# Sixteen neighbourhood heads: score terms stacked on 96 rows, and a mix whose output is feature by token

## The chip, the core and the metric

The kernel runs on one core of one Trainium2 chip. The metric is the device time of one execution, in microseconds (us), as the median of several runs. Engines are named PE (TensorE), ACT (ScalarE), DVE (VectorE), POOL (GpSimd) and SP (SyncE, which issues the weight loads).

## The reference, cut to what matters

The program is a two-block network on 256 tokens of 1024 features, in float32: retention, dilated attention and two feed-forward layers in the first block; a mixer (long convolutions on 512 features, neighbourhood attention on the other 512), a feed-forward layer, a Fourier mix and an eight-expert layer in the second. Only the neighbourhood attention is changed:

```python
def one_row(r):                                  # 16 heads of 32 features, 4 rows of 64 tokens, 256 context keys
    s_loc = einsum('bhjqd,bhrjkd->bhjqrk', q_r, k_r) * scale + bias
    s_loc = where(col_ok, s_loc, NEG_INF)
    s_ctx = einsum('bhjqd,bhcd->bhjqc', q_r, k_ctx) * scale
    p = softmax(concatenate([s_loc, s_ctx]))
    o = einsum('bhjqrk,bhrjkd->bhjqd', p_loc, v_r) + einsum('bhjqc,bhcd->bhjqd', p_ctx, v_ctx)
```

## The kernel before

Every float32 matrix is held in two parts, a high and a low one (`_hi`, `_lo`), and a product of two matrices is three products on PE (`mm3`): high by high, high by low, low by high. ACT makes a high part by copying, DVE makes the low part by subtracting the high one. Weights come in blocks of 1 MB on SP's queue; `ahead` (L1604 on ACT, L2164 on DVE) splits the block that is two ahead of the one in use.

The stage of the change is the neighbourhood attention, interleaved by hand with the projection and the convolution of the other half of the mixer. A loop over the heads h = 0 to 15 is written out for each engine, and each engine works strictly in that order:

- PE, for each head: `nat_turn(h)` transposes the probabilities of both token tiles (8 transposes, L1375); `nat_scores(h + 1)` makes the scores of the next head, per token tile three products of 32 rows and 512 columns (L718 to L720: 256 own keys and 256 context keys); then one block of other work or none; then `nat_mix(h)`, per token tile four products of the high probabilities (64 columns: high and low values side by side, L1388) and four of the low ones (32 columns, L1391). Here the probabilities stand as weights and the values move, so the output is token by feature, in bank 4 of PSUM, four heads side by side.
- The other work: heads 0, 1, 3, 6, 8 and 10 hold a projection block (`z_block`, 48 products of 256 columns); heads 2, 5, 9 and 12 the forward transform of a convolution (`conv_forward`, L1343, 16 products); heads 4, 7, 11 and 13 the way back (`conv_back`, L1355, 16 products); heads 1, 2, 7 and 9 end with four transposes (`conv_turn`, L1328); heads 14 and 15 hold nothing. `conv_forward` waits for the projected rows (`z_middle` on ACT, L1980; `z_sides` on DVE, L2804 and L2809), `conv_back` for DVE's spectrum (`conv_spectrum`, L2821 to L2826).
- ACT: `nat_probs(h)` copies the transposed probabilities as high parts (L2011), `nat_exp(h + 1)` makes the exponentials with their sums (L2002), then `z_middle` (with the split of a weight block, L1612, ahead of it) or `conv_tokens` (L1989); in heads 12 and 14 also high parts of the convolution's result (`conv_high`, L1996).
- DVE: `nat_probs(h)` makes the low parts (L2867), `nat_max(h + 1)` adds the bias and takes the maximum (L2859), then `z_sides`, `conv_spectrum` or `conv_gate`; behind every fourth head `nat_save` adds the two columns of the mix (L2875); in heads 12 and 14 also `conv_low` (L2848).
- POOL: for head h it waits for the maxima of head h - 2, issues two loads of relative biases of 96 KB (L680) and adds the mask (L684); `nat_max(h)` waits for that.

Ahead of the loop ACT and DVE make the high and low parts of the values, `n_v` (L2022, L2886); the first `z_block` waits for them, since it writes the bank that they free. Behind the loop DVE divides by the sums (L2908, L2911), PE transposes the result (8 transposes, L742), ACT and DVE make its parts (`save_fm`), and `accumulate("mix_out", ...)` multiplies by the output weights, first by the convolution's half (two blocks), then by this one.

Of the kernel before, what the change touches and what calls it, by code (L numbers as in the profile page):

```python
# [35 lines left out]
F32 = mybir.dt.float32  # L36
# [4 lines left out]
P = 128  # L41
# [122 lines left out]
def build(nc, a, out):  # L164

    ctx = ExitStack()
    with ctx:
# [13 lines left out]
        h_hi = sb("h_hi", [P, KD, T], FR)  # L181
        h_lo = sb("h_lo", [P, KD, T], FR)
        x_tok = sb("x_tok", [P, TT, D])
# [111 lines left out]
        n_v = over_big("n_v", 14848, 2, 4, HC)  # L295
# [8 lines left out]
        n_pt_lo = h_lo[:, 0:4, :].rearrange("p k t -> p (k t)")  # L304

# [115 lines left out]
        mixed = Signal(sem("mixed"), HEADS)  # L421
        head_saved = Signal(sem("head_saved"), [("att", 2 * AH), ("nat", NH // 2)])
# [280 lines left out]
        def _(pe):  # L703
# [674 lines left out]
            def nat_mix(h, it):  # L1378

                pe.wait_ge(probs_fm.sem, probs_fm.after("nat", 2 * h + it))  # L1380
                if it == 0 and h and h % 4 == 0:
                    pe.wait_ge(head_saved.sem, head_saved.after("nat", h // 2 - 1))
                at = 4 * BANK + h % 4 * P + it * 2 * NHD
                both = psf[:, at:at + 2 * NHD].rearrange("p (a c) -> p a c", a=2)
                c = slice(h * NHD, (h + 1) * NHD)
                for q in range(4):
                    o = it * BANK + q * P
                    mm(both, n_pt_hi[:, o:o + P], n_v[:, :, q, c], start=q == 0, stop=False)  # L1388
                for q in range(4):
                    o = it * BANK + q * P  # L1390
                    last = mm(psf[:, at:at + NHD], n_pt_lo[:, o:o + P], n_v[:, 0, q, c], start=False, stop=q == 3)  # L1391
                last.then_inc(mixed.sem, 1)

# [12 lines left out]
            for h in range(NH):  # L1406
# [14 lines left out]
                nat_mix(h, 0)  # L1421
                nat_mix(h, 1)
# [5 lines left out]
            pe.wait_ge(nat_scaled, TT)  # L1428
            transposes("nat", work, 4, first_bank=6)
# [1816 lines left out]
```

## Time and profile before

| | us |
|---|---|
| median of 3 runs | 2496.03 (2493.82 to 2497.99) |
| profiled execution | 2496.8 |
| its span | 2495.0 |
| mean granted TensorE clock | 0.986 |
| PE busy | 2449.0 (98%) |
| DVE busy | 1910.1 (77%) |
| ACT busy | 1457.5 (58%) |
| POOL busy | 111.3 (4%) |

Busy time is summed over instructions; neighbours on PE overlap, since each one's time includes its latency, so the distance between the starts of two neighbours is what an instruction takes from PE. The clock is a share of full speed: 0.50 is 1.2 GHz, 1.00 is 2.4 GHz.

### The profile page before, as it was taken

To read this page: it belongs to the slowest core of one execution; us is meant where nothing else is said; L and a number is where in the kernel's file an instruction comes from. 1 tells how busy PE (TensorE), PEld (TensorE's weight loads), DVE (VectorE), ACT (ScalarE), POOL (GpSimd) and SP (SyncE) were. 2 spreads that over 40 slices of the span, in tenths; PEclk is the share of its full clock that TensorE was granted. 3 is DMA by queue.
4 is the path that set the end of the run, shared out by engine and by line. 5 is a ranking of instruction groups with operands and counts; after the bars stand their busy time and mean duration, and the time that the engine had idled before them with its cause. 6 is when DMAs were issued, how large, how long until landed. Compare 5 with 4: busy or idle time off the path is not lost.

```text
span 2495.0 us, 35503 instructions
## 1 busy us (share of the span) xinstructions
PE 2449.0 (98%) x12926; PEld 2073.1 (83%) x12926; DVE 1910.1 (77%) x2267; ACT 1457.5 (58%) x1739; POOL 111.3 (4%) x157
## 2 busy tenths in 40 slices
PE   8999999999999999999999999999999999999997
PEld 8787888999987788888788978888888888888886
DVE  6667876555578686466798469999998989899998
ACT  4455443444445344343544458787878787878786
POOL 0000000000010000121110000000000000000000
PEclk9999999999999999999999999999999999999999
DMA  7556766566558753464898359999999999999995
GB/s 249 164 186 220 267 229 191 168 156 156 142 147 286 254 203 109 94 74 49 297 376 301 109 193 355 349 360 350 358 349 361 350 359 351 359 349 359 350 357 217
DMA packets 289140, 633.39 MB, mean 254 GB/s; under 512 B 10843, under 2 KB 72310, under 8 KB 288721
## 3 DMA queue, kind: packets, MB, share of 16 engines
q1 hardware_dynamic: 268512, 556.83, 63.4%
q0 software_dynamic: 20528, 75.17, 12.2%
q8 instruction: 71, 1.16, 0.2%
q14 instruction: 29, 0.23, 0.0%
HBM read 630.82 MB, written 1.14 MB: 253 GB/s over the span
## 4 chain that ended last, share of the span: by engine, by line
PE 93%; DVE 5%; ACT 1%; issue 1%; DMA 1%; DVEq 0%; SPq 0%; ACTq 0%
PE ps L718 28%; PE ps L720 27%; PE ps L719 27%; PE ps L865 1%; DVE w_lo L2170 1%; PE ps L952 1%; PE ps L1343 1%; PE ps L1233 1%; ACT w_hi L1612 1%; PE ps L1097 1%; PE ps L1112 1%; PE ps L1117 1%; PE ps L1355 1%; PE ps L1464 1%; PE ps L742 1%
## 5 line engine op out<-in xcount | busy, mean ns | idle before, releaser
L2170 DVE TENSOR_TENSOR w_lo<-raw,w_hi 128x1024 fp32r<-128x1024 f32 x722 | 874.6, 1225 | 461.3 <-ACT w_hi L1612 439.8
L1612 ACT ACTIVATE w_hi<-raw 128x1024 fp32r<-128x1024 f32 x722 | 755.6, 1059 | 668.7 <-PE ps L720 660.9
L718 PE MATMUL ps<-w_hi,x_hi 128*128 128x512 f32 (+1 forms) x1936 | 742.8, 384 | 5.6 <-DVE x_lo L2187 3.1
L720 PE MATMUL ps<-w_hi,x_lo 128*128 128x512 f32 (+1 forms) x1936 | 726.0, 375 | 0.0
L719 PE MATMUL ps<-w_lo,x_hi 128*128 128x512 f32 (+1 forms) x1936 | 724.8, 374 | 0.0
L718 PEld LDWEIGHTS ps<-w_hi,x_hi 128*128 128x128 f32 x1936 | 365.5, 189 | 89.0 <-issue 17.4
L720 PEld LDWEIGHTS ps<-w_hi,x_lo 128*128 128x128 f32 x1936 | 365.1, 189 | 67.1
L2170 DVE TENSOR_TENSOR w_lo<-big,w_hi 128x1024 fp32r<-128x1024 f32 x336 | 404.2, 1222 | 19.8
L719 PEld LDWEIGHTS ps<-w_lo,x_hi 128*128 128x128 f32 x1936 | 365.9, 189 | 61.6 <-issue 1.0
L1612 ACT ACTIVATE w_hi<-big 128x1024 fp32r<-128x1024 f32 x336 | 357.9, 1065 | 94.3 <-PE ps L720 94.1
L718 PE MATMUL ps<-w_hi,h_hi 128*128 128x512 f32 x760 | 297.2, 391 | 1.1
L719 PE MATMUL ps<-w_lo,h_hi 128*128 128x512 f32 x760 | 295.8, 389 | 0.0
L720 PE MATMUL ps<-w_hi,h_lo 128*128 128x512 f32 x760 | 295.8, 389 | 0.0
L718 PE MATMUL ps<-x_hi,w_hi 128*128 128x256 f32 x672 | 195.6, 291 | 4.5 <-DVE x_lo L2177 2.5
L719 PE MATMUL ps<-x_lo,w_hi 128*128 128x256 f32 x672 | 192.7, 287 | 0.0
L720 PE MATMUL ps<-x_hi,w_lo 128*128 128x256 f32 x672 | 192.7, 287 | 0.0
L718 PEld LDWEIGHTS ps<-w_hi,h_hi 128*128 128x128 f32 x760 | 142.6, 188 | 35.1 <-issue 6.0
L720 PEld LDWEIGHTS ps<-w_hi,h_lo 128*128 128x128 f32 x760 | 142.6, 188 | 29.8
L719 PEld LDWEIGHTS ps<-w_lo,h_hi 128*128 128x128 f32 x760 | 142.7, 188 | 29.1
L718 PEld LDWEIGHTS ps<-x_hi,w_hi 128*128 128x128 f32 x672 | 132.1, 197 | 8.9 <-issue 2.7
L719 PEld LDWEIGHTS ps<-x_lo,w_hi 128*128 128x128 f32 x672 | 132.2, 197 | 0.2 <-issue 0.2
L720 PEld LDWEIGHTS ps<-x_hi,w_lo 128*128 128x128 f32 x672 | 132.0, 196 | 0.0
(402 smaller groups left out, 2202.6 us busy)
## 6 DMA issues: line engine op xcount, KB each, us to landing
raw<-in_moe_w SPq DMA_DIRECT2D x170, 1024.0 KB, 5.1
big<-in_moe_w SPq DMA_DIRECT2D x168, 1024.0 KB, 5.2
big<-in_w_ada POOLq DMA_DIRECT2D x48, 1024.0 KB, 7.7
raw<-in_ffn_w_up SPq DMA_DIRECT2D x44, 1024.0 KB, 5.2
raw<-in_attn_w_in SPq DMA_DIRECT2D x36, 1024.0 KB, 5.0
raw<-in_ffn_w SPq DMA_DIRECT2D x33, 1024.0 KB, 7.2
raw<-in_ret_w_in SPq DMA_DIRECT2D x24, 1024.0 KB, 5.2
raw<-in_ffn_w_down SPq DMA_DIRECT2D x22, 1024.0 KB, 5.0
```

What stands on the lines that cost most here:

```text
L718: mm(dst, lhs[0], rhs[0], start=start, stop=False)
L719: mm(dst, lhs[0], rhs[1], start=False, stop=False)
L720: return mm(dst, lhs[1], rhs[0], start=False, stop=stop)
L742: last = nc.tensor.transpose(ps[:, first_bank + q, o:o + P], src[:, t, c * P:(c + 1) * P], ident)
L865: last = nc.tensor.transpose(psf[:, o:o + P], h_tok[:, t, f * P:(f + 1) * P], ident)
L952: last = mm(ps[:, bank, 2 * f:2 * f + 1], ada_acc(hl, f // 8)[:, c], ones[:, 0:1], start=True, stop=True)
L1097: last = nc.tensor.transpose(psf[:, o:o + P], a_p[:, 384 * it + q * P:384 * it + (q + 1) * P], ident)
L1112: mm(both, a_pt_hi[:, o:o + P], a_v[:, quad % 2, :, j, c:c + AHD], start=q == 0, stop=False)
L1117: last = mm(psf[:, at:at + AHD], a_pt_lo[:, o:o + P], a_v[:, quad % 2, 0, j, c:c + AHD], start=False, stop=q == AG * n - 1)
L1233: last = mm(ps[:, SPECTRUM_BANK[i], :], y_dft[:, part, t, f * P:(f + 1) * P], src, start=t == 0, stop=t == TT - 1)
L1612: nc.scalar.activation(w_hi[:, m % SPLIT, :], raw(SLOT_OF[b])[:, h * HALF:(h + 1) * HALF], ACT.Copy).then_inc(hi_ready, 1)
L2170: V.tensor_tensor(w_lo[:, m % SPLIT, :], raw(SLOT_OF[b])[:, h * HALF:(h + 1) * HALF], w_hi[:, m % SPLIT, :].bitcast(F32), ALU.subtract).th ...
```

## The change

Scores. For heads 1 to 15, ACT issues six DMAs a head, from SBUF to SBUF (`nat_stack`), which lay three parts of 32 rows under each other: of the keys high, high, low (2 KB a row) and of the queries high, low, high (1 KB a row). One product of 96 rows a token tile then makes the same three terms. There are two buffers; head h + 3 is issued in head h, heads 1 and 2 ahead of the loop, and head 2's ahead of the copies of `n_v`. Head 0 stays as it was.

Mix. The values (high and low, 64 columns) stand as weights, and the transposed probabilities of both token tiles (256 columns) move: eight products a head, with the output feature by token on 64 rows of bank 4. ACT copies the 32 rows of the low values' part to their place (`nat_low_part`), DVE adds the 32 rows of the high ones (`nat_sum`), once a head, and PE's next mix waits for that sum. The sums of probabilities are now turned into scales that lie along the tokens: DVE spreads the reciprocals (`nat_scales`), PE transposes them in heads 14 and 15 (`nat_scale_turn`), DVE multiplies (`nat_norm`), ACT and DVE make the parts. The transposes of the result and `nat_save` fall away.

```diff
             def nat_scores(h, it):
...
-                f, r = h // 4, h % 4 * NHD
-                q = [v[r:r + NHD, f, it * P:(it + 1) * P] for v in (n_q_hi, n_q_lo)]
-                k = [v[r:r + NHD, f, :] for v in (n_k_hi, n_k_lo)]
-                mm3(ps[:, it, :], q, k, True, True).then_inc(scored.sem, 1)
+                if h == 0:
...
+                else:
+                    pe.wait_ge(stacked[h % 2], 96 * ((h + 1) // 2))
+                    s = n_stack[h % 2]
+                    mm(ps[:, it, :], s[0:3 * NHD, 2 * T + it * P:2 * T + (it + 1) * P], s[0:3 * NHD, 0:2 * T],
+                       start=True, stop=True).then_inc(scored.sem, 1)
...
+            def nat_mix(h):
+
+                pe.wait_ge(probs_hi.sem, probs_hi.after("nat", 2 * h + 1))
+                if h:
+                    pe.wait_ge(head_saved.sem, head_saved.after("nat", h - 1))
+                dst = ps[0:2 * NHD, 4, 0:T].rearrange("p (t i) -> p t i", t=TT)
+                hi, lo = (v.rearrange("p (t n) -> p t n", t=TT) for v in (n_pt_hi, n_pt_lo))
                 for q in range(4):
...
+                    mm(dst, n_v[:, q, h, :, :], hi[:, :, q * P:(q + 1) * P], start=q == 0, stop=False)
+                pe.wait_ge(probs_fm.sem, probs_fm.after("nat", 2 * h + 1))
                 for q in range(4):
...
+                    last = mm(dst, n_v[:, q, h, :, :], lo[:, :, q * P:(q + 1) * P], start=False, stop=q == 3)
                 last.then_inc(mixed.sem, 1)
+
+            def nat_scale_turn(pair):
+
+                pe.wait_ge(nat_scaled, pair + 1)
+                for f in range(2):
+                    for it in range(TT):
+                        last = nc.tensor.transpose(ps[:, 6 + pair, f * T + it * P:f * T + (it + 1) * P],
+                                                   n_scale[:, pair, it, f * P:(f + 1) * P], ident)
+                last.then_inc(transposed.sem, 1)
...
-                nat_mix(h, 0)
-                nat_mix(h, 1)
+                if h >= 14:
+                    nat_scale_turn(h - 14)
+                nat_mix(h)
...
-            pe.wait_ge(nat_scaled, TT)
-            transposes("nat", work, 4, first_bank=6)
...
+            def nat_stack(h):
+
+                f, r, s = h // 4, h % 4 * NHD, n_stack[h % 2]
+                for i, (k, q) in enumerate(((n_k_hi, n_q_hi), (n_k_hi, n_q_lo), (n_k_lo, n_q_hi))):
+                    rows = slice(i * NHD, (i + 1) * NHD)
+                    nc.scalar.dma_start(s[rows, 0:2 * T].bitcast(F32), k[r:r + NHD, f, :].bitcast(F32)
+                                        ).then_inc(stacked[h % 2], 16)
+                    nc.scalar.dma_start(s[rows, 2 * T:3 * T].bitcast(F32), q[r:r + NHD, f, :].bitcast(F32)
+                                        ).then_inc(stacked[h % 2], 16)
+
+            def nat_low_part(h):
+
+                act.wait_ge(mixed.sem, mixed.after("nat", h))
+                g, r = h // 4, h % 4 * NHD
+                nc.scalar.activation(n_y[r:r + NHD, g // 2, g % 2 * T:(g % 2 + 1) * T], ps[NHD:2 * NHD, 4, 0:T], ACT.Copy
+                                     ).then_inc(nat_part, 1)
+
             nat_exp(0, 0)
             nat_exp(0, 1)
+            nat_stack(1)
             ahead("w_in", 4)
             nat_probs(0, 0)
             nat_probs(0, 1)
             ahead("w_in", 5)
             act.wait_ge(split_free, used("w_in", 5))
+            nat_stack(2)
             for t in range(4):
...
+                if h + 3 < NH:
+                    nat_stack(h + 3)
                 if h in Z_HEAD:
                     z_middle(Z_HEAD.index(h))
...
+                nat_low_part(h)
...
+            def nat_sum(h):
+
+                g, r = h // 4, h % 4 * NHD
+                dve.wait_ge(nat_part, h + 1)
+                y = n_y[r:r + NHD, g // 2, g % 2 * T:(g % 2 + 1) * T]
+                V.tensor_tensor(y, ps[0:NHD, 4, 0:T], y, ALU.add).then_inc(head_saved.sem, 1)
...
+                if h in (13, 14):
+                    nat_scales(h - 13)
+                nat_sum(h)
+                if h == 14:
+                    nat_norm(0)
+            nat_norm(1)
+            for pair in range(2):
+                nat_low(pair)
```

## Rows read from the trace of the kernel before

**Rows 1.** The page: the chain that ended last, shares by engine.
```profile
PE 93%; DVE 5%; ACT 1%; issue 1%; DMA 1%; DVEq 0%; SPq 0%; ACTq 0%
```
**Rows 2.** Windows: stretch, its length, busy time and (instructions) of each engine, PEclk.
```profile
1134.00:1174.00 40.00, 40.00 (x264) 35.11 (x264) 28.28 (x60) 16.84 (x37) 8.87 (x10) 1.00 0.43 45
1176.00:1182.00 6.00, 6.00 (x22) 5.52 (x23) 2.77 (x6) 0.00 (x0) 0.00 (x0) 0.50 0.01 3
```
**Rows 3.** Timeline, PE, head 4: start, busy us, instructions [idle before, releaser].
```profile
1080.27 1.09 PE L1375 MATMUL ps<-sq,hid 128*128 128x128 f32 x8
1081.30 0.50 PE L718 MATMUL ps<-n_k_hi,n_q_hi 32*128 32x512 f32 x1
...
1082.33 0.39 PE L719 MATMUL ps<-n_k_lo,n_q_hi 32*128 32x512 f32 x1
1082.56 0.39 PE L720 MATMUL ps<-n_k_hi,n_q_lo 32*128 32x512 f32 x1
1082.88 3.72 PE L1355 MATMUL ps<-big 128*128 128x256 f32 x16
1086.25 0.72 PE L1388 MATMUL ps<-n_v,h_hi 128*128 128x64 f32 x4
...
1088.14 1.09 PE L1375 MATMUL ps<-sq,hid 128*128 128x128 f32 x8
```
**Rows 4.** Timeline, PE, head 3: first product of the projection block, first of the mix.
```profile
1072.72 0.39 PE L718 MATMUL ps<-x_hi,w_hi 128*128 128x256 f32 x1
...
1078.57 0.53 PE L1388 MATMUL ps<-n_v,h_hi 128*128 128x64 f32 x4
```
**Rows 5.** Timeline, PE: the instructions after a wait, and the first mix_out product.
```profile
1040.41 0.58 PE L718 MATMUL ps<-x_hi,w_hi 128*128 128x256 f32 x1 [2.02 <-DVE n_v L2886]
...
1064.44 3.69 PE L1343 MATMUL ps<-big 128*128 128x256 f32 x16 [0.72 <-DVE big L2809]
...
1128.44 5.14 PE L1343 MATMUL ps<-big 128*128 128x256 f32 x16 [1.12 <-issue]
...
1175.97 1.06 PE L1388 MATMUL ps<-n_v,h_hi 128*128 128x64 f32 x4 [1.13 <-DVE h_lo L2867]
...
1179.41 0.77 PE L718 MATMUL ps<-w_hi,x_hi 128*128 128x512 f32 x1
```
**Rows 6.** Timeline, ACT: the copies of n_v, then head 1 up to the split.
```profile
1036.83 1.06 ACT L1612 ACTIVATE w_hi<-raw 128x1024 fp32r<-128x1024 f32 x1 [3.88 <-PE ps L720]
1037.80 2.04 ACT L2022 ACTIVATE n_v<-ps 128x512 fp32r<-128x512 f32 x4
...
1057.50 0.71 ACT L2002 ACTIVATE hid<-hid,a_stat 128x512 f32<-128x512 f32 x1
...
1059.15 2.00 ACT L1612 ACTIVATE w_hi<-raw 128x1024 fp32r<-128x1024 f32 x2 [0.85 <-PE ps L720]
```
**Rows 7.** Timeline, DVE: z_sides' last piece in head 1, a spectrum in head 5.
```profile
1063.42 0.87 DVE L2809 SCALAR_TENSOR_TENSOR big<-ps,cols,big 128x255 f32<-128x255 f32 x2
...
1094.51 0.69 DVE L2821 TENSOR_TENSOR big<-ps,big 128x512 f32<-128x512 f32 x1 [2.54 <-PE ps L1343]
...
1098.23 1.28 DVE L2867 TENSOR_TENSOR h_lo<-ps,h_hi 128x512 fp32r<-128x512 f32 x2
```
**Rows 8.** Line L466, SP's issues of the output weights: ns min/median/max of one.
```profile
L466 SPq DMA_DIRECT2D raw<-in_w_mix_out x4: 367/368/368, 1062.6 to 1126.7; - x4
```
**Rows 9.** Lines, 1034 to 1185 us: count, busy us, mean ns of one, idle before.
```profile
L680 POOL DMA_DIRECT2D big<-in_na_rpb x26 | 17.1, 663 | 37.7 <-DVE a_stat L2859 21.8 <-issue 15.8
L684 POOL TENSOR_TENSOR big<-big,hid 128x384 f32<-128x384 f32 x13 | 15.6, 1200 | 69.0 <-DMA big<-in_na_rpb 69.0
...
L2848 DVE TENSOR_TENSOR x_lo<-big,x_hi 128x256 fp32r<-128x256 f32 x4 | 1.5, 419 | 1.3 <-ACT x_hi L1996 1.3
L1996 ACT ACTIVATE x_hi<-big 128x256 fp32r<-128x256 f32 x4 | 1.4, 400 | 0.0
```
**Rows 10.** DMA issues, 1034 to 1185 us: count, KB each, median us to landing.
```profile
big<-in_na_rpb POOLq DMA_DIRECT2D x26, 96.0 KB, 5.6
```

More of the change, by code:

```diff
@@ L294, in build @@
         n_k_lo = over_big("n_k_lo", 12800, 4, 2 * T)
-        n_v = over_big("n_v", 14848, 2, 4, HC)
+        n_v = over_big("n_v", 14848, 4, NH, 2, NHD)
         n_bias = carve(18944, 2, 384)
@@ L304, in build @@
         n_pt_lo = h_lo[:, 0:4, :].rearrange("p k t -> p (k t)")
+        n_stack = [nc.alloc_sbuf_tensor_at("n_stack0", [P, 3 * T], FR, offset=h_hi_at + 4 * 4 * T),
+                   nc.alloc_sbuf_tensor_at("n_stack1", [P, 3 * T], FR, offset=hid_at + 4 * 1408)]
+        n_scale = nc.alloc_sbuf_tensor_at("n_scale", [P, 2, TT, T], F32, offset=h_lo_at + 4 * 4 * T)
+        n_y = work[:, :, 0:HC]
         def n_bias_of(h, it):
@@ L420, in build @@
         probs_fm = Signal(sem("probs_fm"), HEADS)
-        mixed = Signal(sem("mixed"), HEADS)
-        head_saved = Signal(sem("head_saved"), [("att", 2 * AH), ("nat", NH // 2)])
+        mixed = Signal(sem("mixed"), [("att", 2 * AH), ("nat", NH)])
+        head_saved = Signal(sem("head_saved"), [("att", 2 * AH), ("nat", NH)])
+        stacked = [sem(f"stacked{i}") for i in range(2)]
+        nat_normed = sem("nat_normed")
+        nat_part = sem("nat_part")
         probs_hi = Signal(sem("probs_hi"), HEADS)
@@ L2020, in _ @@
             act.wait_ge(split_free, used("w_in", 5))
+            nat_stack(2)
             for t in range(4):
-                nc.scalar.activation(n_v[:, 0, t, :], in_bank(6 + t), ACT.Copy).then_inc(in_hi, 1)
+                nc.scalar.activation(n_v[:, t, :, 0, :], in_bank(6 + t).rearrange("p (h c) -> p h c", h=NH), ACT.Copy
+                                     ).then_inc(in_hi, 1)
             for h in range(NH):
@@ L2036, in _ @@
                     conv_high(h // 2 - 6)
-            save_fm("nat", 2, first_bank=6, k0=4, rows=reversed_rows)
+                nat_low_part(h)
+            for pair in range(2):
+                act.wait_ge(nat_normed, pair + 1)
+                nc.scalar.activation(reversed_rows(x_hi[:, 4 + 2 * pair:6 + 2 * pair, :]),
+                                     n_y[:, pair, :].rearrange("p (a i) -> p a i", i=P), ACT.Copy
+                                     ).then_inc(fm_hi.sem, 1)
             for b in range(3):
@@ L2885, in _ @@
                 dve.wait_ge(in_hi, 6 + t + 1)
[L2886 to L2887 removed]
+                V.tensor_tensor(n_v[:, t, :, 1, :], in_bank(6 + t).rearrange("p (h c) -> p h c", h=NH),
+                                n_v[:, t, :, 0, :].bitcast(F32), ALU.subtract).then_inc(proj_saved.sem, 1)
             for h in range(NH):
@@ L2901, in _ @@
                     conv_gate(BACK_HEAD.index(h))
-                if h % 4 == 3:
-                    nat_save(h // 4)
                 if h in (12, 14):
                     conv_low(h // 2 - 6)
-            dve.wait_ge(probs.sem, probs.after("nat", 2 * NH - 1))
-            dve.wait_ge(head_saved.sem, head_saved.after("nat", NH // 2 - 1))
-            link(V.reciprocal(a_stat[:, 4:6, :], a_stat[:, 2:4, :]))
-            for t in range(TT):
-                w = work[:, t, 0:HC].rearrange("p (h c) -> p h c", h=NH)
-                V.tensor_tensor(w, w, a_stat[:, 4 + t, :].unsqueeze(2).broadcast_to([P, NH, NHD]), ALU.mult
-                                ).then_inc(nat_scaled, 1)
-            save_fm("nat", 2, first_bank=6, k0=4, rows=reversed_rows)
+                if h in (13, 14):
[4 more added lines that the diff above has]
+            nat_norm(1)
+            for pair in range(2):
+                nat_low(pair)
             for b in range(3):
```

43 lines of the change are left out of this document (23 added, 20 removed).

## The prediction

> **What bounds the kernel now.** I read the chain that ended last first: TensorE (PE) holds 93% of the span [rows 1], so time leaves the kernel where PE works less and nothing else is late. The change touches one stage, the sixteen neighbourhood heads, from about 1031 to 1179 us. The table of windows shows PE busy 40.0 of 40.0 us in its middle at full clock, ScalarE (ACT) 16.8 and VectorE (DVE) 28.3 [rows 2]. So PE bounds the stage, but DVE at 70% is not far behind. Then I read the timelines of PE, ACT and DVE head by head, for two things: the spacing of PE's instructions (their starts; a busy time of one includes its latency), and how early the other engines' results come.
>
> One head of PE work, head 4 at full clock [rows 3]: eight transposes 1080.27 to 1081.30 (1.03 us), six score products to 1082.88 (1.58; spacing 0.23 for 512 columns), a convolution block to 1086.25 (3.37), sixteen mix products to 1088.14 (1.89). In heads with a projection block instead, 48 products of 256 columns take 5.85 us, 0.122 each [rows 4].
>
> PE waits few times, but waits of about 1 us and more are followed by a low clock [rows 5]. After 2.02 us (1040.41) the products of 256 columns ran 0.21 apart; after 1.12 us (1128.44) the block of 16 took 5.14 where its peers take 3.7 with their latency [rows 3, 5]; after 1.13 us (1175.97) the mix took 3.44 for 1.70 and the next products 0.43 for 0.23, with granted clock 0.50, which is 1.2 of 2.4 GHz [rows 2, 5]. A wait of 0.72 (1064.44) was followed by none [rows 5]. The price of these stretches: 2.4 us (26 products by 0.09), 1.4, and 2.9 (1.7 on the mix, 6 by 0.20); mean 2.2.
>
> **The change, part by part.**
> Scores: heads 1 to 15 run two products for six. Time goes by columns and not by rows (512 columns on 32 rows 0.23, 256 on 128 rows 0.122 [rows 3, 4]), so 96 rows cost the same: 4 x 0.233 x 15 = 14.0 us less of PE.
> Mix: eight products of 256 columns for sixteen, 8 x 0.122 + 0.19 of switching = 1.17 for 1.89 [rows 3, 4]: 0.72 x 16 = 11.5 us less.
> The eight transposes of the outputs become eight of the scales, 1.0 us either way, only earlier [rows 3]: nothing.
> In all 25.5 us less PE work. It is all won only if PE is never late for others.
>
> Against it stand these.
> (a) Start. The six transfers of head 2 are issued on ACT ahead of its n_v copies, which began at 1037.80 right behind the split at 1036.83 [rows 6]; PE's first projection block waited for their low parts until 1040.41 [rows 5]. No DMA is issued on ACT before. The nearest row is SyncE's: 0.367 us each [rows 8]; GpSimd's 0.663 [rows 9] is the upper bound, near nothing the lower. I take 0.37, the same kind of issue by a hardware queue. Six are 2.2 us; the 1.0 us split runs beside them, so 1.3 late (0 to 3.0).
> (b) Head 2. After projection block 1, conv_forward waits for ACT's and DVE's work on z. The split began at 1059.15 and the convolution at 1064.44, 5.3 later, with DVE's last piece starting 1063.42 [rows 5 to 7]. Now ACT dispatches the second exponential at 1057.50 + 1.3 and issues six transfers: 61.0, the convolution at 66.3 at the latest. PE came at 1063.72; 1.3 later at the start, less two scores (0.93) and two mixes (0.72), that is 61.7. It waits some 4.4 instead of 0.7. Lost 3.7.
> (c) Head 9 is the same pair (projection block 4, then conv_forward): 1.12 before [rows 5], now 1.1 plus what two heads save less what ACT's issues take: about 3.3. Lost 2.2.
> (d) Heads 4-5, 7-8 and 11-12. Behind a projection block DVE splits (2.3), does z (1.7), the new sum, the low parts (1.2) and the maxima (1.2), then ACT's exponentials; PE needs them two heads later, and arrives 3.3 earlier than now. Walking the three engines through it with the rows' durations, PE waits 1.6, 1.5 and 1.6.
> (e) Head 13. DVE's spectrum takes 3.72 (1094.51 to 1098.23 [rows 7]) from the end of head 12's convolution; PE fills that with mix 1.17, transposes 1.03 and scores 0.66: 1.5 late with the two hand-overs.
> (f) Heads 14 and 15 have no block to hide in. PE goes at the pace of transposes, high parts, low parts, maxima, exponentials; DVE also has the scales and the first normalisation there. Waits of 5.0 for 1.1: lost 3.9.
> (g) The new copy on ACT is at most 0.40 a head and the sum on DVE 0.42 (the rows of 256 columns at 128 partitions, L1996 and L2848 [rows 9]). ACT's copy waits for the mix; behind it stand the next head's high parts, which wait for transposes that come 1 us after the mix anyway. DVE's sum stands ahead of the next low parts and ends before their high parts do: nothing, except what is in (d) and (f).
> (h) GpSimd's bias rows for head h start after head h-2's maxima and take two issues, 5.6 to landing and 1.2 of addition, 8.1 at most [rows 9, 10]; serial, that is less than the 8.7 a head that PE takes now (1040.41 to 1179.41 over sixteen [rows 5]) and than the 8.3 after. The walk finds them late in no head; they begin to cost from about 9.0 a head.
> (i) Tail. The last head goes copy, sum, normalise, high, low, about 3.5 us, beside two weight blocks of mix_out (24 products each, 11 us): nothing.
>
> Sum: 25.5 - 1.3 - 3.7 - 2.2 - 4.7 - 1.5 - 3.9 = 8.2 us at an equal clock. The clock: before's own stretches at 1128 and 1176 (1.4 + 2.9 = 4.3) stand at places that wait anyhow, so I count all anew: four waits of 1.1 us and more (heads 2, 9, 13, 15) by 2.2 = 8.8, of which 1.4 is absorbed, since what head 13's stretch delays would wait in 14 and 15 too. 8.2 + 4.3 - 8.8 + 1.4 = 5.1 us. From the profiled execution's 2496.8 (span 2495.0) to 2491.7; the median of the runs, 2496.0, is 0.8 under it, so 2490.9.
>
> A rule to weigh against (a). The rows show 0.367 us for one issue [rows 8]. The Trainium skill, "DMA: Bandwidth & Descriptors", section "Anatomy of one DMA — SWDGE (gpsimd) path", puts the dispatch by the sequencer at about 50 ns; by it (a) is gone and (b) 1.4 shorter. The sum would be 8 to 9 us and not 5. The trace disagrees for SyncE and says nothing of ACT.
>
> **The rivals.**
> A, no low clock behind the new waits. For: 0.72 went unpunished and the stretch of 1128 was short [rows 5]. Against: three of three waits over 1.1 were followed by one. 8.2 + 4.3 = 12.5 less: 2483.5.
> B, low clock longer and from 1.0 us on. Then the waits of 1.06 in heads 5 and 11 have one too, and each costs 2.9 as at 1176: six by 2.9 = 17.4, 3 of it absorbed; 14.4 - 8.2 - 4.3 = 1.9 more than before: about 2498, no measurable change.
> C, slower: the issue on ACT costs what it does on GpSimd, 0.66, or the transfers hold ACT's queue that long. Six are 4.0 us a head on an engine on which (a), (b), (c) and (d) hang: the start 3.0 late, and each projection pair later by the 1.8 more. The walk gives 14 us over before: 2510. It decides from about 0.5 us an issue; at that the gain is gone. For: no row of ACT issuing. Against: SyncE's 0.367 in every one of its rows.
> D, issue near nothing: 9 us less, 2487.
>
> **How the numbers follow.** The forecast 0.39, A 0.13, D 0.10, B 0.25, C 0.13. What a measurement of this kernel can tell from no change is about 0.2%, 5.0 us, so the forecast lies on that bound: half of its case and a little more (0.24) with A and D give 0.47 faster; its other half (0.15) with B's larger part (0.21) 0.36 within; C and B's rest 0.17 slower. The likeliest case alone reaches from 2487 to 2495. The range leaves out the far end of C and values under A: 2483 to 2501.
>
> **What would show it.** Issues on ACT of 0.37 us (a, C). The first n_v copy 1.3 later behind the split, and PE's first wait over 4 us. Two score products 0.23 apart and eight mix products 0.12 apart (more than 0.14 would take 2.5 us of the gain). Waits at conv_forward of heads 2 and 9 of 3 to 4.5 us, at conv_back of head 13 of 1.5, and a granted clock of 0.5 behind them. From the first projection block to the first mix_out product: 139.0 before, 132.6 after. Wrong would be: issues dearer than 0.5, bias rows landing so late that the maxima wait for GpSimd, low clock in most heads.

## The result, and the profile after

The changed kernel takes 2504.27 us (2503.84 to 2508.23, 6 runs) beside 2495.91 us (2492.1 to 2498.05, 6 runs) for the kernel before: ratio 1.0037, 95% interval 1.0025 to 1.005. It is slower by 8.4 us (by the ends of the interval 6 to 12). The forecast of 2490.9 us, and its range up to 2501, were wrong. The profiled execution took 2504.08 us with a span of 2502.2.

| | before | after |
|---|---|---|
| profiled execution, span (us) | 2496.8, 2495.0 | 2504.08, 2502.2 |
| first projection block to first mix_out product (us) | 139.00 | 146.17 |
| of it PE busy, PE idle (us) | 136.03, 2.97 | 116.93, 29.24 |
| granted TensorE clock in it | 0.95 | 0.87 |

From the page of the changed kernel, its busy times, a queue and the chain that ended last, which answers to [rows 1]:

```profile
PE 2428.1 (97%) x12738; PEld 2055.7 (82%) x12738; DVE 1915.3 (77%) x2280; ACT 1464.7 (59%) x1755; POOL 110.5 (4%) x157
...
q10 hardware_dynamic: 4320, 4.43, 0.6%
...
PE 90%; DVE 6%; issue 1%; ACT 1%; ACTq 1%; DMA 0%; DVEq 0%; SPq 0%
```

PE has gone from 93% to 90% of the chain, and ACTq is in it: ScalarE's queue, which does nothing there but issue transfers. The queue q10 is new; its 4.43 MB are the 90 stack transfers.

Windows over the stage, first of the kernel before, then of the changed one; the columns are those of [rows 2]:

```profile
1040.41:1179.41 139.00, 136.03 (x893) 121.80 (x893) 88.18 (x178) 58.99 (x122) 32.47 (x39) 0.95 0.54 72
```
```profile
1041.36:1187.53 146.17, 116.93 (x717) 104.34 (x717) 94.56 (x194) 65.89 (x138) 31.62 (x39) 0.87 0.56 91
```

Here is the whole case. PE's work fell by 19.1 us (136.03 to 116.93), and its idle time rose by 26.3 (2.97 to 29.24). The change did what it says and more than gave it back in waits. DVE and ACT are busy only 6 and 7 us more: nobody is overloaded. Somebody is late.

Timeline of PE in the changed kernel, the longest waits and what came behind them, as in [rows 5]:

```profile
1041.36 0.58 PE L727 MATMUL ps<-x_hi,w_hi 128*128 128x256 f32 x1 [5.32 <-DVE n_v L2955]
...
1067.92 5.27 PE L1352 MATMUL ps<-big 128*128 128x256 f32 x16 [7.02 <-DVE big L2856]
...
1089.64 0.66 PE L1400 MATMUL ps<-h_hi,n_v 128*64 128x256 f32 x4 [2.24 <-DVE work L2922]
1090.86 0.68 PE L1403 MATMUL ps<-h_lo,n_v 128*64 128x256 f32 x4 [0.57 <-DVE h_lo L2914]
1092.32 1.97 PE L1389 MATMUL ps<-sq,hid 128*128 128x128 f32 x8 [0.78 <-ACT hid L2022]
...
1116.72 0.65 PE L1400 MATMUL ps<-h_hi,n_v 128*64 128x256 f32 x4 [2.67 <-DVE work L2922]
...
1136.26 5.24 PE L1352 MATMUL ps<-big 128*128 128x256 f32 x16 [5.90 <-issue]
...
1157.94 0.65 PE L1400 MATMUL ps<-h_hi,n_v 128*64 128x256 f32 x4 [2.24 <-DVE work L2922]
...
1187.53 0.63 PE L727 MATMUL ps<-w_hi,x_hi 128*128 128x512 f32 x1
```

Read the brackets from the top: 5.32 us at the first projection block (2.02 before [rows 5]), 7.02 at conv_forward of head 2 (0.72 before), 5.90 at that of head 9 (1.12 before), and three mixes, of heads 4, 7 and 11, that wait 2.2 to 2.7 us for DVE's sum of the head before.

PE is only the victim. The timeline of ACT and its queue in head 1 shows who made it wait:

```profile
1058.19 0.72 ACT L2022 ACTIVATE hid<-hid,a_stat 128x512 f32<-128x512 f32 x1 [3.73 <-DVE a_stat L2906]
1058.81 0.51 ACTq L2039 DMA_DIRECT2D n_stack<-n_k_hi  x1
...
1058.92 0.71 ACT L2022 ACTIVATE hid<-hid,a_stat 128x512 f32<-128x512 f32 x1
1059.36 0.61 ACTq L2041 DMA_DIRECT2D n_stack<-n_q_hi  x1
...
1061.92 0.61 ACTq L2041 DMA_DIRECT2D n_stack<-n_q_hi  x1
1062.64 2.00 ACT L1632 ACTIVATE w_hi<-raw 128x1024 fp32r<-128x1024 f32 x2 [2.92 <-issue]
```

The issues begin just as the second exponential goes to the engine (1058.81), come 0.64 us apart and end at 1062.53. The split starts at 1062.64, and the profile names nothing else that it waited for. Before, it started 1.65 us after the second exponential [rows 6], now 3.72. ACT stands idle for 2.92 us meanwhile; `issue` is the reason given. The waits of the stage hold all such places (in all, how many, the longest):

```profile
ACT w_hi L1632 <- issue: 14.6, 5, 2.9
...
ACT work L2048 <- issue: 8.6, 3, 2.9
...
ACT big L2009 <- issue: 2.9, 1, 2.9
ACT x_hi L2016 <- issue: 2.9, 1, 2.9
```

Ten times ScalarE stands idle for 2.9 us behind issues: ahead of five splits of a weight block, three copies of the low part, one `conv_tokens` and one `conv_high`. How the first kind reaches PE two engines on is seen in heads 3 and 4, in the timelines of ACT and DVE (it ends at PE's mix of 1089.64, above):

```profile
1083.90 2.01 ACT L1632 ACTIVATE w_hi<-raw 128x1024 fp32r<-128x1024 f32 x2 [2.92 <-issue]
```
```profile
1084.99 2.36 DVE L2217 TENSOR_TENSOR w_lo<-raw,w_hi 128x1024 fp32r<-128x1024 f32 x2 [4.95 <-ACT w_hi L1632]
1087.26 0.87 DVE L2851 SCALAR_TENSOR_TENSOR big<-ps,cols,big 128x255 f32<-128x255 f32 x2
1088.17 0.87 DVE L2856 SCALAR_TENSOR_TENSOR big<-ps,cols,big 128x255 f32<-128x255 f32 x2
1089.07 0.42 DVE L2922 TENSOR_TENSOR work<-ps,work 32x256 f32<-32x256 f32 x1
```

ACT's part of the split comes 2.9 us late, DVE waits 4.95 us for it, then does its own part of the split, its part of z and the sum without a pause, and PE's mix waits 2.24 us for the last of them. The label at PE names the sum, which took 0.42 us; the cause is the issues that began 9 us earlier (1080.08).

### The profile page after: what moved, and what is told of

It reads as the page before. It is cut to its first block, busy times and chain, and to the rows that moved or that the text cites. A ratio compares the mean times of both kernels' runs of the same rounds, so it can differ in the third digit from the quotient of the medians.

```text
span 2502.2 us, 35289 instructions
## 1 busy us (share of the span) xinstructions
PE 2428.1 (97%) x12738; PEld 2055.7 (82%) x12738; DVE 1915.3 (77%) x2280; ACT 1464.7 (59%) x1755; POOL 110.5 (4%) x157
## 3 DMA queue, kind: packets, MB, share of 16 engines
q10 hardware_dynamic: 4320, 4.43, 0.6%
## 4 chain that ended last, share of the span: by engine, by line
PE 90%; DVE 6%; issue 1%; ACT 1%; ACTq 1%; DMA 0%; DVEq 0%; SPq 0%
PE ps L727 27%; PE ps L729 26%; PE ps L728 26%; PE ps L874 1%; DVE w_lo L2217 1%; PE ps L1352 1%; PE ps L961 1%; ACT w_hi L1632 1%; PE ps L1106 1%; PE ps L1121 1%; PE ps L751 1%; PE ps L1126 1%; PE ps L1484 1%; PE ps L1242 0%; DVE h_lo L2538 0%
```

## The experiments

**Theory T.** An issue of these transfers holds ScalarE's queue 0.64 us, not 0.37; six a head make 3.8 us, on an engine whose results PE needs soon. **Rival Q:** the traffic itself, or the stacks landing late. **Rival R:** the new mix (64 columns of weights, a chain of accumulation with a wait in it, low clock behind its waits).

The first four runs, side by side (before 2496.09 us beside them).

**e1, the issues moved to SyncE.** The six transfers of a head stand between weight loads, behind waits that hold them to the same places in time; nothing else changes.

```diff
-                    nc.scalar.dma_start(s[rows, 0:2 * T].bitcast(F32), k[r:r + NHD, f, :].bitcast(F32)
+                    sp.wait_ge(negmax.sem, ...)           # head 2: split_free
+                    sp.dma_start(s[rows, 0:2 * T].bitcast(F32), k[r:r + NHD, f, :].bitcast(F32)
```

> The changed kernel with its six transfers a head issued on SyncE instead of ScalarE, between the weight loads, at the same points in time; nothing else is changed. Theory T (the issues on ScalarE, 0.64 us each in the trace of the changed kernel, hold that engine 3.8 us a head, and the blocks behind it come late): the first projection block starts 2.2 us sooner, PE's waits at conv_forward of heads 2 and 9 fall from 7.0 and 5.9 us to 2 to 3, and the whole is 3 to 9 us faster than before, 12 to 17 faster than changed. Rival R (the loss comes from the new mix and its hand-over from PE to ScalarE to VectorE, and from the low clock): within 3 us of the changed kernel, 2501 to 2507. Rival Q (the transfers' traffic delays the bias rows and weights): as changed too, with landing of the bias rows at 5.8 us or more.

Measured: 2486.41 us, ratio 0.9966 (0.9955 to 0.9978). That is 9.7 us faster than before and 18 faster than the change, with the same transfers and the same bytes. Its windows row over the stage, and PE's wait in head 2:

```profile
1039.24:1173.09 133.85, 114.29 (x717) 100.63 (x718) 95.52 (x194) 65.48 (x137) 32.12 (x39) 0.92 0.67 104
```
```profile
1062.65 6.72 PE L1372 MATMUL ps<-big 128*128 128x256 f32 x16 [4.02 <-DVE big L2862]
```

Idle time falls from 29.2 to 19.6 us. The stacks now come late in two heads (0.8 and 0.3 us of PE); more of Q doesn't show at PE. The waits in heads 2 and 9 are 4.0 and 3.1 us, not the 2 to 3 expected. Most of the first has nothing to do with issues: PE waited 0.72 us there before, and comes 3.3 us earlier by the two scores and two mixes that it saves ahead of it, together 4.0. The queue of SyncE tells why the forecast's price was wrong:

```profile
1058.99 0.59 SPq L469 DMA_DIRECT2D n_stack<-n_k_lo  x1
1059.63 0.59 SPq L471 DMA_DIRECT2D n_stack<-n_q_hi  x1
1060.84 0.37 SPq L495 DMA_DIRECT2D raw<-in_w_mix_out  x1
```
```profile
1039.38 0.58 SPq L495 DMA_DIRECT2D raw<-in_w_in  x1
```

The same engine takes 0.59 us for a stack transfer and 0.37 for a weight load, so the price doesn't hang on who issues it. But two things differ between these rows. The load of 0.37 stands alone, 0.6 us behind the last issue. The one weight load that stands directly behind a stack issue (the row of 1039.38; the issue ahead of it ended at 1039.33) took 0.58 us, and it did so in every run with all six transfers on SyncE. The kernel before shows it too, in three weight loads issued one behind the other (line L466, ns min/median/max, as in [rows 8]):

```profile
L466 SPq DMA_DIRECT2D raw<-in_moe_w x3: 367/506/507, 1446.3 to 1447.2; - x3
```

The first takes 0.37 us, the next two 0.51. The first stack transfer of a row of six takes 0.51, the others 0.59. So both count: the kind of transfer and, more than I saw, that six issues stand in a row. What the move buys is that nothing urgent stands behind SyncE's issues.

**e2, the new mix alone.** Scores as before, no stacks, no issues on ACT.

```diff
-                    pe.wait_ge(stacked[h % 2], 96 * ((h + 1) // 2))
-                    mm(ps[:, it, :], s[0:3 * NHD, ...], s[0:3 * NHD, 0:2 * T], start=True, stop=True)
+                mm3(ps[:, it, :], q, k, True, True)
```

> The new mix alone: scores are made as before, by three products of 32 rows, and nothing is stacked. T: no issue on ScalarE, so no long wait; of the 11.5 us of PE work that the mix saves about half remains behind the other engines' pace, 5 us faster than before (2489 to 2494). R: slower than before by most of the changed kernel's 8 us (2500 or more).

Measured: 2492.22 us, ratio 0.9989 (0.998 to 0.9997): 3.9 us faster by the medians, 2.7 by the ratio. R falls: the new mix, with its chain, its copy and its sum, costs nothing by itself where nothing is issued on ScalarE.

**e3, the stacked scores alone**, issued on ScalarE, with the mix of the kernel before.

```diff
-                mm3(ps[:, it, :], q, k, True, True)
+                    pe.wait_ge(stacked[h % 2], 96 * ((h + 1) // 2))
+                    mm(ps[:, it, :], s[0:3 * NHD, ...], s[0:3 * NHD, 0:2 * T], start=True, stop=True)
+                nat_stack(h + 3)        # on ScalarE, behind the exponentials
```

> The stacked scores alone, issued on ScalarE as in the changed kernel: the mix and all behind it as before. T: slower than before by about 6 us (4 to 9), since the issues are there and the work that they save is 14 us of PE's at most. R: faster than before by 3 or more, as the mix is the old one.

Measured: 2501.58 us, ratio 1.0027 (1.0016 to 1.0038), 5.5 us slower by the medians, 6.7 by the ratio. The loss comes in with the issues on ScalarE. e2 and e3 add up to +1.6 us by the medians and the change has +8.4: what the new mix saves of PE's work is worth nothing where PE waits anyhow. Whether it even costs something there, since its copies stand behind the issues too (8.6 us of ScalarE's idle time above), isn't shown: the intervals of e3 and of the change overlap.

**e4, the change without the transfers of heads 3 to 15.** Their scores are made from what heads 1 and 2 left in the buffers, so its output is not the reference's.

```diff
-                if h + 3 < NH:
-                    nat_stack(h + 3)
-                    pe.wait_ge(stacked[h % 2], 96 * ((h + 1) // 2))
+                    pe.wait_ge(stacked[h % 2], 96)
```

> The changed kernel without the transfers of heads 3 to 15: their scores are made from what heads 1 and 2 left in the two buffers, so the values are not the reference's, while all other instructions and waits stay. T: between the changed kernel and the one with issues on SyncE: the late start of 2.2 us stays, the waits of heads 2 and 9 go, 2490 to 2496. R: as changed. Q, the traffic: faster than the one with issues on SyncE by 2 or more, since that has the traffic and this has not.

Measured: 2486.75 us, ratio 0.997 (0.996 to 0.9979). It equals e1, which moves all the bytes, so Q falls. Its first wait is still the 5.3 us of the change, since the transfers of head 2 are still issued ahead of the n_v copies; its waits in heads 2 and 9 are e1's, 4.0 and 3.1 us. T's own expectation (2490 to 2496, and these waits gone) missed on both counts: the waits are those of the saved work, as in e1, and the late start, which was to cost 2.2 us over e1, shows no cost here.

The next four runs, side by side (before 2495.87 us beside them).

**e5, scores on SyncE with the old mix:** e3 with e1's edit.

```diff
-                    nc.scalar.dma_start(...)      # of e3
+                    sp.dma_start(...)             # between weight loads, as e1
```

> The score part alone, with its transfers issued on SyncE, and the mix of the kernel before (sixteen products a head, transposes of the outputs at the end). Set against e1 it gives what the new mix is worth on top. My reading (waits decide, not TensorE's work): the waits on VectorE and ScalarE in heads 2 and 9 are the limit of the first half, so the old mix fills waits that e1 has; with 14.0 us less of score products and waits of 2 to 3 us in heads 2 and 9 it is 6 to 8 us faster than before, 2488 to 2490. The rival, that both parts add up (e1 has 25.5 us less TensorE work and gained 9.7, so its mix part would bring its share, 11.5 of 25.5 of it), puts it at 5.3 us faster, 2490.8. If it reaches e1's 2486.4 or less, the new mix brings nothing on top.

Measured: 2488.62 us, ratio 0.997 (0.9959 to 0.998): 7.2 us faster, as the first expectation had it. Its stage has 120.64 us of PE work and 9.17 idle, that of the same kernel with the new mix (e12, below) 111.84 and 18.87: the 8.8 us less work turn into 9.7 us more idle time. Whether the new mix brings anything on top of e5 isn't shown; the intervals overlap.

**e6, head 2's transfers behind the n_v copies.**

```diff
             act.wait_ge(split_free, used("w_in", 5))
-            nat_stack(2)
             for t in range(4):
                 nc.scalar.activation(n_v[:, t, :, 0, :], ...)
+            nat_stack(2)
```

> The changed kernel with one thing moved: the six transfers of head 2 are issued on ScalarE behind its four n_v copies and not ahead of them. Theory T (each issue holds ScalarE's queue 0.64 us): the first n_v copy starts 1.0 us behind the split as before, TensorE's first wait falls from 5.3 to about 3.1 us, and the stage, which hangs on that start, ends 2.2 us earlier: 2502. The other waits stay (7.0 in head 2, 5.9 in head 9). If the later waits take the start back (they hang on ScalarE's own order and not on TensorE), the time stays at 2504 and the wait in head 2 grows by the 2.2 us.

Measured: 2500.62 us, ratio 1.0028 (1.0017 to 1.004): 2.2 us less than the change by the ratios, 3.7 by the medians, with intervals that overlap; the trace says more. PE's first wait is 3.14 us, that of head 2 stays long (6.37). ACT and its queue:

```profile
1032.75 1.06 ACT L1632 ACTIVATE w_hi<-raw 128x1024 fp32r<-128x1024 f32 x1 [3.87 <-PE ps L729]
1032.77 0.52 ACTq L2039 DMA_DIRECT2D n_stack<-n_k_hi  x1
...
1033.72 0.58 ACT L2060 ACTIVATE n_v<-ps 128x512 fp32r<-128x512 f32 x1
```

The first issue starts at 1032.77 although four copies stand ahead of it in the program: the queue had already handed them over and ran on. Issues behind work whose inputs are ready run beside it. Issues ahead of it hold it up.

**e7, nine issues for six:** each key transfer in two halves of 256 columns.

```diff
-                    nc.scalar.dma_start(s[rows, 0:2 * T].bitcast(F32), k[r:r + NHD, f, :].bitcast(F32)
+                    for c in (slice(0, T), slice(T, 2 * T)):
+                        nc.scalar.dma_start(s[rows, c].bitcast(F32), k[r:r + NHD, f, c].bitcast(F32)
```

> The changed kernel with each key transfer cut into two halves of 256 columns: nine issues a head for six, the same bytes and the same places. Theory T: what counts is the number of issues at 0.6 us each, so ScalarE is held 5.8 us a head for 3.8, its copies and exponentials come 1.9 later, and a walk through the engines' orders gives 17 us over the changed kernel, 2521 (2515 to 2527), with the waits in heads 2 and 9 near 8 to 9 us. If the cost of an issue went by its bytes or its descriptors' length, an issue of half the size would take 0.3 us, and the time would stay at 2504 to 2506.

Measured: 2532.39 us, ratio 1.0156 (1.0142 to 1.017), 28 us over the change. T's direction, but more than its 17. Three issues more are 1.92 us a head, 28.8 over fifteen heads: all of it is lost. The first six are cheaper: by e4, 13 heads of them cost 17.5 us for 49.9 us of issuing. The likely reason is that they still use time that ACT had to spare, and that the further three find none. The rows of the issues (least, median and longest, in ns), first of the change, then of e7:

```profile
L2039 ACTq DMA_DIRECT2D n_stack<-n_k_hi x30: 514/612/616, 1018.9 to 1168.9; - x30
L2041 ACTq DMA_DIRECT2D n_stack<-n_q_hi x30: 608/612/862, 1019.5 to 1170.8; - x30
```
```profile
L2040 ACTq DMA_DIRECT2D n_stack<-n_k_hi x60: 514/612/918, 1020.6 to 1197.3; - x60
```

Half the bytes, the same 612 ns. In the change the row of L2039 is of 2 KB and that of L2041 of 1 KB on each of 32 rows: 612 ns again.

**e8, e1 with the waits of heads 2 and 9 filled.**

```diff
                 pe.wait_ge(tok_saved, s + 1)
+                if s in (0, 2):
+                    for i in range((30, 24)[s // 2]):
+                        mm(ps[:, 5, 0:T], y_dft[:, 0, 0, 0:P], y_dft[:, 1, 0, :], start=True, stop=True)
```

> e1 (transfers issued on SyncE) with 30 and 24 further products of 256 columns, whose results nobody reads, on TensorE between its two waits ahead of conv_forward in heads 2 and 9, where it would stand idle 4.0 and 3.1 us. It measures what the low clock behind these waits costs. In e1 the 16 products behind the wait in head 2 took 6.7 us, where they take 3.7 at full clock, and the granted clock over the next 10 us was 0.86. If the time so saved is kept: 3 to 5 us less than e1, 2482. If the later waits on ScalarE and VectorE take it back: within 1 us of e1, 2486, with longer waits in heads 3 to 8. If the products themselves end later than the awaited work, it is slower than e1 by up to 1 us.

Measured: 2497.11 us, ratio 1.0009 (0.9998 to 1.002), 10.7 over e1. My error: these products took 0.44 us each, as those of the convolution do, not 0.12 (each leaves two records: a convolution block, which the text ahead gives 16 products, is 8 products, the x16 rows of 3.7 us), so that 54 are 23.8 us for 7.1 us of waiting. It says nothing on the low clock; e10 mends it.

The next three runs (before 2494.81 us beside them).

**e9, three issues on each engine:** keys on SyncE, queries on ScalarE, at the same time.

```diff
-                    nc.scalar.dma_start(s[rows, 0:2 * T].bitcast(F32), k[...])
+                    sp.dma_start(s[rows, 0:2 * T].bitcast(F32), k[...])      # as e1
                     nc.scalar.dma_start(s[rows, 2 * T:3 * T].bitcast(F32), q[...])
```

> The changed kernel with the transfers of each head divided: the three of the keys are issued on SyncE as in e1, the three of the queries on ScalarE as in the changed kernel. ScalarE is then held three times 0.64 us, 1.9 us a head, nearly the 2.2 us (six times 0.37) of the forecast. It tests whether the rest of the forecast was right once its issue time is given to it. Theory T: the time of the forecast, 2491 (2489 to 2494), waits of about 4 to 5 us in head 2 and 3 to 4 us in head 9. If the loss comes in above some hold a head that 1.9 us already passes: over 2496. If only the last of it counts and 1.9 us hide: e1's 2486.

Measured: 2489.79 us, ratio 0.9979 (0.997 to 0.9988): 5.0 us faster by the medians, where the forecast had 5.1. The row over its stage, and its waits in heads 2 and 9:

```profile
1037.60:1170.64 133.04, 113.52 (x716) 100.59 (x717) 95.96 (x194) 65.98 (x138) 31.18 (x39) 0.91 0.67 104
```
```profile
1060.58 6.27 PE L1370 MATMUL ps<-big 128*128 128x256 f32 x16 [4.71 <-DVE big L2872]
...
1121.40 6.58 PE L1370 MATMUL ps<-big 128*128 128x256 f32 x16 [4.47 <-issue]
```

A stage of 133.0 us (forecast 132.6), with 19.5 us idle (the forecast's waits sum to 18.9). The second of ScalarE's three issues took longer than any usual one of the change, while SyncE issued too:

```profile
1053.67 0.87 ACTq L2057 DMA_DIRECT2D n_stack<-n_q_lo  x1
```

From the first issue to the end of the third it is 2.07 us a head, not 1.9. That is near the 2.2 that the forecast assumed, and the time is the forecast's. The support is weaker than it looks, though. e1 issues nothing on ScalarE, and its stage, in one execution each, is no shorter (133.9 us, 19.6 idle; 130.7 and 18.9 in e12, below). By the ratios e9 lies 3.2 us over e1 and 4.5 over e12, and the intervals just overlap. Taken together the runs give a clear order: ScalarE held 0, 2.1, 3.8 and 5.8 us a head gives ratios of 0.9966, 0.9979, 1.0037 and 1.0156. The first 2 us cost little, the next 1.7 cost 14.

**e10, the fill of e8 with 8 and 6 products;** then **e12 and e13,** e1 and e10 again side by side (before 2496.89 us beside them).

```diff
-                    for i in range((30, 24)[s // 2]):
+                    for i in range((8, 6)[s // 2]):
```

> e8 over again with a fill of the right length. The products that it put in front of conv_forward took 0.44 us each and not 0.12 (the 60 records of 13.2 us in e8 are its 30 products and conv_forward's own), so that 30 of them ran past the wait by over 9 us. Now 8 in head 2 (3.5 us for a wait of 4.0 in e1) and 6 in head 9 (2.6 us for 3.1). Their results are read by nobody. If what is saved of the low clock is kept: 3 to 5 us less than e1, a ratio to before of 0.995. If later waits take it back: e1's ratio, 0.9966.

> e1 once more, side by side with e10's kernel, to tell what the filled waits are worth: e1 and e10 were timed beside different runs of before, 0.9966 and 0.9970 with intervals of 0.0011 to either side, while the stage took 133.9 us in the one profiled execution and 127.7 in the other. If the fill is worth what the stages say, this one lies 3 to 6 us over e13; if it is given back behind the stage or the executions only differ among themselves, both lie within 1.5 us.

> e10 once more, side by side with e1's kernel (e12). 3 to 6 us under e12 if the low clock behind the waits in heads 2 and 9 costs what the forecast took (two stretches of 2.2 us) or more; within 1.5 us of it if not.

Measured: e10 2487.09 us, ratio 0.997 (0.996 to 0.9981); e12 2486.05 us, ratio 0.9961 (0.9948 to 0.9975); e13 2489.22 us, ratio 0.9965 (0.9952 to 0.9977). e12 and e13 lie 1 us apart by the ratios: the fill brings nothing that can be measured. What comes behind PE's waits in head 2, in e12 the convolution (L1372), in e10 the fill (L1366) and the convolution (L1375), in e13 the fill:

```profile
1062.92 5.13 PE L1372 MATMUL ps<-big 128*128 128x256 f32 x16 [4.01 <-DVE big L2862]
```
```profile
1058.12 3.72 PE L1366 MATMUL ps<-big 128*128 128x256 f32 x16 [1.49 <-ACT big L2032]
1061.67 3.62 PE L1375 MATMUL ps<-big 128*128 128x256 f32 x16
```
```profile
1063.82 5.41 PE L1366 MATMUL ps<-big 128*128 128x256 f32 x16 [2.16 <-ACT big L2032]
```

e1 and e12 are the same kernel, and this block takes 6.72 us in the one execution and 5.13 in the other, behind the same wait of 4.0: over 3.72, that is 3.0 and 1.4 us. So a stretch of low clock has no fixed price. e10 and e13 are the same kernel, and the fill itself ran at full speed in the one (3.72, behind 1.49 us) and not in the other (5.41, behind 2.16). The convolution behind it took 3.62 us in both, and that of head 9 3.72, for 5.4 in e1 and 5.2 in e12: there the fill did take the low clock away. In head 2 it also came too late. It begins only when ScalarE has the tokens ready, and DVE's last piece was done at 1059.81 in e10 and at 1065.52 in e13, while the convolution started at 1061.67 and 1069.06: 1.9 and 3.5 us lost to the fill. So these runs don't show what taking the low clock away would be worth. The stages of e1, e12, e10 and e13 took 133.9, 130.7, 127.7 and 131.3 us.

**e11, what sets the time of an issue.** Three more transfers inside SBUF on each engine, of 128 rows, 32 rows and one row.

```diff
+                    (n_stack[0][:, 0:128], n_k_hi[:, 0, 0:128]),
+                    (n_stack[0][0:32, 128:256], n_k_hi[0:32, 1, 0:128]),
+                    (n_stack[0][64:65, 128:256], n_k_hi[64:65, 2, 0:128]),
```

> e1 with three further SBUF to SBUF transfers of 128 columns behind head 15's exponentials on ScalarE, and the same three on SyncE: of 128 rows, of 32 rows and of one row. It looks at what sets the time of an issue. If the rows (and so the pieces that the transfer is cut into) set it, 128 rows take over 1 us and one row under 0.4. If it is a fixed price of a transfer inside SBUF, all take 0.5 to 0.64 us on both engines. The kernel's own time is up by some us through ScalarE's wait for them.

The rows of the three on ScalarE, in that order, and the three together on SyncE:

```profile
1156.96 1.80 SPq L491 DMA_DIRECT2D n_stack<-n_k_hi  x3
...
1162.72 0.56 ACTq L2096 DMA_DIRECT2D n_stack<-n_k_hi  x1
1163.32 0.61 ACTq L2096 DMA_DIRECT2D n_stack<-n_k_hi  x1
1163.95 0.61 ACTq L2096 DMA_DIRECT2D n_stack<-n_k_hi  x1
```

128 rows 0.56 us, one row 0.61: the rows don't raise the price, and the 0.05 less is that of a first issue in a row, as in e1. So far the record has, on SyncE: a weight load 0.37 us alone and 0.51 to 0.58 directly behind another issue, a transfer inside SBUF 0.51 as the first of a row and 0.59 within it. A single transfer inside SBUF with nothing near it, and a load from memory issued by ScalarE, weren't tried. The time, in one run, is e1's (2487.74 us).

## Why the prediction was wrong

In the profiled executions the span grew by 7.2 us where the forecast had it shrink by 5.1. Ahead of the stage it is 0.95 longer (forecast 1.3), in it 7.2 longer (forecast 6.4 shorter), behind it 0.9 shorter (forecast nothing): the miss lies in the stage, 13.6 us, of which 10.3 are idle time of PE; the other 3.3 are PE's busy time, for which low clock is the only cause seen.

| step | forecast | measured | in e9 |
|---|---|---|---|
| issue on ACT (us, and a head) | 0.37, 2.2 | 0.64, 3.8 | 2.1 a head |
| (a) first wait of PE | over 4 | 5.32 | 3.65 |
| (b) wait in head 2 | 4.4 | 7.02 | 4.71 |
| (c) wait in head 9 | 3.3 | 5.90 | 4.47 |
| (d) heads 4-5, 7-8, 11-12 | 1.6, 1.5, 1.6 | 3.6, 3.5, 3.6 | 1.9, 1.2, 1.9 |
| (e) head 13 | 1.5 | 1.63 | 1.64 |
| (f) heads 14 and 15 | 5.0 | 3.95 | 3.0 |
| idle in the stage, sum of (b) to (f) | 18.9 | 29.2 | 19.5 |

**The step that failed** is the price in (a): "I take 0.37, the same kind of issue by a hardware queue". The rows behind it [rows 8] are weight loads of 1 MB from memory, each issued alone. The change issues six transfers inside SBUF, one directly behind the other, and measured 0.64 us from start to start. I took likeness of queue for likeness of transfer, and one issue for a row of six. The kernel before had no row of a transfer inside SBUF on these queues, but it had the second thing: weight loads in a row at 0.51 (the line of L466 under e1). GpSimd's 0.663 [rows 9] I used only as the upper end. At 0.27 us more, six issues are 1.6 us more a head. An estimate from the prediction's own two points, 5.1 us less at 0.37 and 14 more at 0.66 (C), puts 0.64 at some 13 over before on a straight line; measured were 8.4, so the rest of the working was too dear there rather than too cheap. Rival C named this mechanism, and put the point where the gain is gone at 0.5 us an issue; it had 0.13. Its argument against ("SyncE's 0.367 in every one of its rows") was the same mistake, and not true of all of SyncE's rows, only of those shown. D's price of free issues, 9 us less, is what e1 gave (9.7).

The Trainium skill, "DMA: Bandwidth & Descriptors", section "Issuing engines are not separate DMA queues", says that issuing on several engines only saves the sequencer's time to start a transfer, "which is usually small relative to the DMA itself". The comparison itself holds here: 0.61 us beside a median of 4.8 us from issue to landing. What one might take from it, that the saving doesn't matter, does not: moving 90 issues from one queue to another changed the time by 18 us (e1). The Trainium skill, "Perfetto Trace Analysis", section "DMA Instruction — HWDGE (DVE, Sync)", has the issue's row in a profile end when the sequencer is free for its next instruction; by that the rows of 0.61 us are time for which all behind them waits, and the split that starts 0.11 us after the sixth row agrees.

**Right in the work.** Forecast 25.5 us less at an equal clock, 0.9 of it ahead of the stage. PE's busy time in the stage fell by 19.1 with the clock at 0.87, by 24.7 in e4 and 24.2 in e12 with 0.93: what the change lacks to 24.6 goes with the lower clock. The spacings are as forecast. Timeline of PE, head 0's mix to head 2's scores:

```profile
1049.79 0.63 PE L1400 MATMUL ps<-h_hi,n_v 128*64 128x256 f32 x4
1050.26 0.63 PE L1403 MATMUL ps<-h_lo,n_v 128*64 128x256 f32 x4
1050.73 1.03 PE L1389 MATMUL ps<-sq,hid 128*128 128x128 f32 x8
1051.52 0.72 PE L1379 MATMUL ps<-n_stack 96*128 96x512 f32 x2
```

Eight mix products start 0.94 us ahead of what follows (forecast 1.17, the 0.19 of switching isn't there), and 96 rows cost what 32 did: the two score products take 0.56 us to the next instruction, where the last two of the six took 0.55 [rows 3].

**(a) to (c)** right in mechanism and place, each too short. In (b) the convolution started at 1067.92, 1.6 us behind the forecast's 66.3, which is what six dearer issues add; the other 1.0 of the wait is mostly PE, which came at 1060.90 and not at 61.7. The n_v copies began 3.8 us behind the split, not 1.0 + 1.3, and PE's first product 5.7 us behind it, for 3.6 before.

**(d)** right in its chain (split, z, sum, low parts, maxima on DVE), which is the one shown above; three waits of 3.5 us for 1.6 because its first link, ACT's split, stands behind the issues. In e9, with half the issues, they are 1.9, 1.2 and 1.9.

**(g)** right in its result, not in its reason. I looked at what stands behind the copy. Ahead of it, in heads 4, 7 and 11, stand the six issues alone, and it comes 2.9 us late three times. It costs PE nothing there because a convolution block covers it: the mix of head 5 started at 1099.93 without a wait, 3.3 us after the sum. The cover is not in the text of the forecast, as it should have been.

**(e), (f), (h), (i)** (e) right to 0.1 us in its wait, but see the clock. (f) too high by 1.0. (h) right: bias rows landed in 5.8 us for 5.6 [rows 10], and in no head did DVE's maxima wait for GpSimd. (i) right: what follows the stage took 1314.67 us, before 1315.59.

**The clock.** Four stretches at 2.2 us, in heads 2, 9, 13 and 15. Low clock did follow the waits of heads 2 and 9 (granted 0.68 and 0.69 over the 5 us behind them) and the last wait of head 15 (0.66 over the next 4.5 us, mostly behind the stage). Behind the wait of head 13 there was none, at a granted clock of 1.00:

```profile
1172.48 3.72 PE L1364 MATMUL ps<-big 128*128 128x256 f32 x16 [1.63 <-DVE big L2873]
```

And it followed the waits of heads 4, 7 and 11 (0.67 to 0.71), which the forecast didn't count. So the places were wrong in four of seven, and e1 beside e12 shows that the price of one differs between executions of one kernel (3.0 and 1.4 us). PE's busy time in e9's stage is 113.5 us where the forecast's stage less its waits leaves 113.7, so the sum came out about right there; with parts that are wrong that is luck, and their prices are not shown.

**The chances.** The issue's price was unknown between near nothing and 0.66, and C decided from 0.5. A range "0 to 3.0" for (a) stood in the text, but the range of the time took in only the near part of what the same price does in (b), (c) and (d). Carried through, its upper end was 2510, and the measured 2504 lies inside.

## What to carry to other kernels

An issue is an instruction on its engine like any other: price it by a row of the same kind of transfer, issued alone or in a row as yours will be, and if there is none, let the dearest row of any kind decide whether the engine that PE waits for may issue it. Put small transfers on a queue behind which nothing urgent stands, or behind work whose inputs are ready; here that made 2504 into 2486 us, 0.3 to 0.4% faster than the kernel before (e1, e12), with the arithmetic of the change untouched. And where the engine that is bound loses work, walk the engines that feed it first: of 25 us less work on PE, the best version kept 10.

## What the hardware showed unexpectedly

- The time of an issue hardly hangs on how much is moved: nearly always 0.51 to 0.61 us for transfers inside SBUF with 1, 32 or 128 rows, with 128, 256 or 512 columns, from ScalarE and from SyncE. It hangs on what was issued just before it: 1 MB from memory on SyncE took 0.37 us alone, 0.51 directly behind one like it, and 0.58 behind a transfer inside SBUF. When both engines issued at once (e9), ScalarE's second took 0.87.
- While its queue issues, ScalarE finishes only what it had been handed. It stood idle for 2.9 us with its input ready. In e6 the split and four copies had been handed over by the time of the first issue, so that six issues cost nothing.
- Low clock behind a wait is not a constant of the program: the same convolution block behind the same 4.0 us wait took 6.72 and 5.13 us in two executions of one kernel (e1, e12), and in e5's execution the blocks behind waits of 2.23 and 2.24 us took 3.69, full speed, and 5.38.
